# Identity products in TensorE's waits, and one full-array product for the sample rows of a window

## The reference

```
x = x + gt1 * mix
h = rms_norm(x, norm_ffn_w) * (1 + sc2) + sh2
group  = argmax(h @ w_group_router)              # 1 of 4 groups
top-2  = 2 best of the group's 8 experts         # 32 experts in all
y      = sum over the 2 experts of  weight * (silu(h @ gate) * (h @ up)) @ down     # FF = 256
x = x + gt2 * y
out = rms_norm(x, final_norm_w) * (1 + scale) + shift
```

## Time and profile before

| | us |
|---|---|
| median of 3 runs (range) | 838.47 (837.27 to 840.47) |
| profiled execution, its own time | 839.85 |
| span of its trace | 838.1 |
| TensorE busy, share of the span | 728.8, 87% |
| VectorE, ScalarE, GpSimd busy | 264.0, 195.1, 97.5 |
| mean granted TensorE clock | 0.942 |

### The profile page before, as it was taken

The page is one execution under the profiler, slowest core; times in us unless marked ns, Lnnn a source line. Parts: engine busy times, 40 slices in busy tenths (PEclk is TensorE's granted clock), DMA queues, the critical chain, the costliest instruction groups (busy, mean ns, idle before and its releaser), DMA issues.

```text
span 838.1 us, 19950 instructions
## 1 busy us (share of the span) xinstructions
PE 728.8 (87%) x8393; PEld 529.4 (63%) x8394; DVE 264.0 (32%) x737; ACT 195.1 (23%) x500; POOL 97.5 (12%) x229
## 2 busy tenths in 40 slices
PE   2779999999988975998988999973998989999985
PEld 1567777787766654776766777733655656656554
DVE  0145412430134350666683112144111111111122
ACT  1221113112731322122223200051111112121225
POOL 7000000001011222100000000001212221222200
PEclk9869999999999996999998999985899999999996
DMA  7835579999444954651002706875899999999901
GB/s 264 228 103 201 201 245 327 327 327 334 121 112 122 260 148 103 200 179 26 1 2 74 266 0 268 334 300 204 313 413 411 414 413 411 415 412 414 385 15 56
DMA packets 108728, 195.88 MB, mean 234 GB/s; under 512 B 9964, under 2 KB 71097, under 8 KB 100488
## 3 DMA queue, kind: packets, MB, share of 16 engines
q1 hardware_dynamic: 106760, 189.94, 63.1%
q0 software_dynamic: 1920, 5.25, 1.7%
HBM read 185.40 MB, written 9.77 MB: 233 GB/s over the span
## 4 chain that ended last, share of the span: by engine, by line
PE 81%; DVE 6%; DMA 4%; issue 4%; ACT 3%; SPq 1%; POOL 0%; ACTq 0%; DVEq 0%; POOLq 0%
PE ps L1142 17%; PE ps L533 10%; PE ps L1212 7%; PE ps L506 5%; PE ps L546 5%; PE ps L430 4%; PE ps L451 4%; PE ps L1084 4%; PE ps L509 3%; PE ps L434 2%; PE ps L496 2%; DMA arena<-in_w_ada 1%; SPq L811 1%; PE ps L540 1%; DVE arena L1894 1%
## 5 line engine op out<-in xcount | busy, mean ns | idle before, releaser
L1142 PE MATMUL ps<-arena 128*128 128x288 f32 x576 | 144.8, 411 | 0.0
L1142 PEld LDWEIGHTS ps<-arena 128*128 128x128 f32 x576 | 109.3, 192 | 31.2 <-issue 1.0
L533 PE MATMUL ps<-arena 128*32 128x128 f32 x2432 | 86.7, 278 | 15.3 <-issue 12.8
L533 PEld LDWEIGHTS ps<-arena 128*32 128x32 f32 x2432 | 69.3, 111 | 39.4 <-issue 38.2
L1212 PE MATMUL ps<-arena 128*128 128x288 f32 x256 | 76.2, 427 | 14.2 <-DMA arena<-in_w_in 10.3
L1212 PEld LDWEIGHTS ps<-arena 128*128 128x128 f32 x256 | 45.3, 194 | 30.1 <-DMA arena<-in_w_in 10.6
L506 PE MATMUL ps<-level,arena 32*128 32x256 f32 x624 | 44.8, 401 | 0.5 <-DVE arena L775 0.5
L546 PE MATMUL ps<-arena,hact 128*32 128x256 f32 x608 | 40.7, 385 | 0.0
L770 DVE TENSOR_TENSOR h_row<-h_row,ps 128x64 f32<-128x64 f32 x38 | 8.4, 221 | 96.6 <-ACT h_row L628 96.6
L404 POOL DMA_INDIRECT arena<-h_rows,idx_now x38 | 37.6, 988 | 9.5 <-issue 9.5
L1084 PE MATMUL ps<-arena,cT 128*32 128x128 f32 x1024 | 33.8, 292 | 4.6 <-DMA arena<-in_w_ada 4.6
(11 more groups left out here) (432 smaller groups left out, 983.0 us busy)
## 6 DMA issues: line engine op xcount, KB each, us to landing
arena<-in_w_exp_gate SPq DMA_DIRECT2D x32, 1024.0 KB
arena<-in_w_exp_up SPq DMA_DIRECT2D x32, 1024.0 KB
arena<-in_w_exp_down SPq DMA_DIRECT2D x32, 1024.0 KB
arena<-in_w_ada SPq DMA_DIRECT2D x12, 2048.0 KB, 10.2
arena<-in_w_in SPq DMA_DIRECT2D x18, 1024.0 KB, 5.9
arena<-in_w_ada_final SPq DMA_DIRECT2D x4, 2048.0 KB, 14.9
arena<-in_w_in SPq DMA_DIRECT2D x16, 512.0 KB, 4.7
arena<-in_state_ssm_rec SPq DMA_DIRECT2D x8, 512.0 KB, 6.0
```

The source lines that it names most:

```text
L533: l = mm(ps[CW * q:CW * (q + 1), 5, 0:P].rearrange("p (g f) -> p g f", g=2), xwin[:, at:at + CW], gate_up[:, :, k, f:f + HF], start=(k == ...
L1142: l = mm(ps[:, 2 + 2 * sl + m, 0:TOK], w_ring[sl][:, k, m * P:(m + 1) * P], HN[:, k, :], start=(k == 0), stop=(k == KT - 1))
```

## The change

Three edits. A helper busy(n, bank) does n products of the identity with itself taken twice (128 x 128 by 256 columns, fp32) into a bank that nobody reads. It is called before the pair counts (4, after the wait for the last h2_tok, which moves here from below), after the counts (13), after the lists (7), after the last two transposes of y_row (4), and after the final sums of squares (10).

In combined() the four 32 x 32 products of L509 become one product of 128 contraction rows by 128 columns. For that the sample part of PT becomes four times 32 columns, block-diagonal, so PT has 384 columns in place of 288. The table iota has the prompt's numbers, then four blocks of the sample tokens' numbers, in which GpSimd sets to -1 all that is not in a partition of the block's own quarter (two affine_select). The small tables behind them move, and slot_tab takes the place of LG.

```diff
--- before.py
+++ after.py
@@ -267,11 +267,12 @@
         h_row = sb("h_row", [P, HF])
         hact = sb("hact", [P, HF])
         late = level[:].rearrange("p l n -> p (l n)")
-        PT, iota = late[:, 0:TOK], late[:, TOK:2 * TOK]
-        LG = late[:, 2 * TOK:2 * TOK + 108].rearrange("p (t x) -> p t x", t=3)
-        slot_tab = late[:, 2 * TOK + 108:2 * TOK + 108 + 2 * NWIN].rearrange("p (a w) -> p a w", a=2)
-        tid = late[:, 800:806].rearrange("p (c t) -> p c t", c=2)
-        quarter = late[:, 806:807]
+        PTW = SEQ + 4 * SMP
+        PT, iota = late[:, 0:PTW], late[:, PTW:2 * PTW]
+        LG = late[:, 2 * PTW:2 * PTW + 108].rearrange("p (t x) -> p t x", t=3)
+        slot_tab = late[:, 2 * PTW:2 * PTW + 2 * NWIN].rearrange("p (a w) -> p a w", a=2)
+        tid = late[:, 2 * PTW + 108:2 * PTW + 114].rearrange("p (c t) -> p c t", c=2)
+        quarter = late[:, 2 * PTW + 114:2 * PTW + 115]
         idx = sb("idx", [P, NWIN], I32)
         idx_now = sb("idx_now", [P, 2], I32)
         idx_seen = sb("idx_seen", [1, 1], I32)
@@ -389,7 +390,12 @@
             e.wait_ge(S("y_out"), 6)
             e.wait_ge(S("o_out"), 3)
             e.wait_ge(S("x2"), KT)
-            link(g.iota(iota, pattern=[[1, TOK]], base=0, channel_multiplier=0, allow_small_or_imprecise_dtypes=True))
+            link(g.iota(iota[:, 0:SEQ], pattern=[[1, SEQ]], base=0, channel_multiplier=0, allow_small_or_imprecise_dtypes=True))
+            own = iota[:, SEQ:PTW].rearrange("p (m t) -> p m t", t=SMP)
+            link(g.iota(own, pattern=[[0, 4], [1, SMP]], base=SEQ, channel_multiplier=0, allow_small_or_imprecise_dtypes=True))
+            for step, base in ((-SMP, 0), (SMP, SMP - 1)):
+                link(g.affine_select(out=own, in_=own, pattern=[[step, 4], [0, SMP]], base=base,
+                                     channel_multiplier=1 if step < 0 else -1, compare_op=ALU.is_ge, fill=-1.0))
             link(g.iota(tid, pattern=[[0, 2], [P, 3]], base=0, channel_multiplier=1, allow_small_or_imprecise_dtypes=True))
             link(g.memset(LG, 0.0))
             for q in range(4):
@@ -480,6 +486,14 @@
                         l = tr(ps[0:p_, 5, u * 36:(u + 1) * 36], lg_row[:, o_:o_ + p_], ident[0:EG + E, 0:EG + E])
                     l.then_inc(S("rt_mm"), 1)
 
+            def busy(n, bank):
+
+                for _ in range(n):
+                    mm(ps[:, bank, 0:2 * P].rearrange("p (a c) -> p a c", a=2), ident[:, :],
+                       ident[:, :].unsqueeze(1).broadcast_to([P, 2, P]), start=True, stop=True)
+
+            e.wait_ge(S("h2_tok"), 6)
+            busy(4, 7)
             e.wait_ge(S("routed"), 2)
             for t in range(3):
                 for u in range(t):
@@ -488,6 +502,7 @@
             for t in range(3):
                 l = mm(ps[:, 5, 3 * E:4 * E], ones[:, :], r_eq[:, t, :], start=(t == 0), stop=(t == 2))
             l.then_inc(S("count_mm"), 1)
+            busy(13, 7)
 
             def picked_transposed(n):
 
@@ -504,12 +519,9 @@
                     for m in range(4):
                         r = slice(CW * m, CW * (m + 1))
                         mm(ps[:, m, j * SEQ:(j + 1) * SEQ], y_row[r, j * P:(j + 1) * P], PT[r, 0:SEQ], start=False, stop=last and j == 1)
-                for m in range(4):
-                    r = slice(CW * m, CW * (m + 1))
-                    l = mm(ps[r, 4, 0:2 * P], PT[r, SEQ:TOK], y_row[r, :], start=False, stop=last)
+                l = mm(ps[:, 4, 0:2 * P], PT[:, SEQ:PTW], y_row[:, :], start=False, stop=last)
                 l.then_inc(S("comb_mm"), 1)
 
-            e.wait_ge(S("h2_tok"), 6)
             for a in range(2):
                 e.wait_ge(S("placed"), a + 1)
                 for i in range(6):
@@ -517,6 +529,7 @@
                     for q in range(4):
                         l = mm(ps[CW * q:CW * (q + 1), 6 + a, 0:NWIN], B6[0:p, i, :], AV[0:p, a, i, :], start=(i == 0), stop=(i == 5))
                 l.then_inc(S("count_mm"), 1)
+            busy(7, 5)
             picked_transposed(0)
             e.wait_ge(S("comb_mm"), 1)
 
@@ -569,9 +582,11 @@
             for j in range(2):
                 l = tr(ps[:, 5, j * P:(j + 1) * P], y_row[:, j * P:(j + 1) * P], ident[:, :])
             l.then_inc(S("xt_mm"), 1)
+            busy(4, 7)
             for k in range(KT):
                 e.wait_ge(S("x3"), k + 1)
                 mean_square(3, k, 6)
+            busy(10, 7)
             e.wait_ge(S("y_fin"), 1)
             e.wait_ge(S("x_mod"), 3 * KT)
             for t, (o, p) in enumerate(TILES):
@@ -769,7 +784,7 @@
                 e.wait_ge(S("h_silu"), c + 1)
                 tt(h_row[:], h_row[:], ps[:, 5, HF:P], ALU.mult).then_inc(S("h_row"), 1)
                 e.wait_ge(S("comb_mm"), c + 2)
-                ts(PT, iota[:, 0:TOK], slot_tab[:, 0, bass.ds(c, 1)], slot_tab[:, 1, bass.ds(c, 1)], ALU.is_equal,
+                ts(PT, iota, slot_tab[:, 0, bass.ds(c, 1)], slot_tab[:, 1, bass.ds(c, 1)], ALU.is_equal,
                    ALU.mult).then_inc(S("pt"), 1)
                 e.wait_ge(S("down_mm"), c + 1)
                 v.tensor_copy(y_row, ps[:, 7, 0:2 * P]).then_inc(S("y_row"), 1)
```

## The result

The changed kernel takes 841.0 us in the median of 20 runs, the kernel before 838.25 in 20: ratio 1.0031, 95% interval 1.0019 to 1.0043. I forecast 831.0, a gain of 7.5 us, with a range of 826 to 838. It is slower by 2.6 us (1.6 to 3.6). That is less than the 4.2 us that I had set as the least clear difference, so by my own classes it is "within", to which I gave 20%; but the time lies outside my range, and the sign is wrong. They are taken from fast executions alone, which all are but one of full_rows_only's seven, at 1767.13 us.

A forecast was written before the change was run, and what follows sets the result against it. TensorE's chain was taken as the bound, slowed by half-rate clock stretches in the tail. Tables +1.0, held clock -7.25 and sample product -1.2 gave -7.45 us, from 838.47 to 831.0 us; range 826 to 838.

The forecast's parts named there:

- the price of the sample product: L509's replacement in each window: 0.60 us in place of 0.63, a gain of 0.03 in each of 39, 1.2 us.
- the first window: First expert window at full clock: L533 falls from 3.64 to 2.43, gain 1.2 us, and 0.1 from L506.
- L518: no gain: Lists: 35 ns an instruction at half rate against 38 ns for L533 at full rate, so a held clock gains nothing.
- The tables: GpSimd's chain ahead of the router: an iota and two affine_select add 1.0 us, and all the routing moves by that.
- Counts: Pair counts, 18 instructions: 4.05 us at half rate, 1.9 at full rate, a gain of 2.1 us.
- Final norm: Tail end: final squares 6.94 against 4.1, gain 2.8 us; final transposes and copies, gain 0.8 us.
- my first rival: Level falls in the counts all the same: 2.1 us lost, lists 1.8 late, 834.9 us; chance 20%.
- my own upper bound: Sample product in each window: if its weight load doesn't hide, 0.70 us, a loss of 0.07, 2.7 in all.
- the "no gain" that I worked out by it: Sample product by the skill's tiling rule: the drains are as many, the gain is nothing, 832.2 in place of 831.0 us.
- My other bound: Sample product: if the weight load hides entirely, it costs only 0.46 us, up to 0.13 gained, 5.1 in all.
- the cover is ... the gather: Identity products cost nothing at full rate, covered by VectorE's routing work, the gather, the root and the modulation.
- my second rival: Ahead of the router: the level's rise of 557.0 comes later, L468 ends 3.9 us late, 833.9 us; chance 10%.

The follow-up runs named there:

- full_rows_only: Kernel before with one edit: L462 takes all 128 contraction rows of y_row and xT in place of 32; 837.14 us, ratio 0.9952.
- load_and_tables: Changed kernel with expert 6's down weights loaded after the gathered rows are copied and the new tables made behind the clearing of y_row; 834.75 us, ratio 0.9962.
- fills_loop: Kernel before with all 38 identity products as counted loops, old sample product, tables and load order; 837.37 us, ratio 0.9977.
- load_after_gather: Changed kernel in which SP asks for expert 6's down weights only when ScalarE has copied the first gathered rows; 838.55 us, ratio 0.9989.
- tables_late: Changed kernel with GpSimd's three new table instructions moved behind the clearing of y_row; 839.01 us, ratio 1.0016.
- fills_only: Kernel before with all 38 identity products written out, old sample product and tables; 870.65 us, ratio 1.0377.
- product_only: Changed kernel without its five busy() calls: full-array sample product, wider PT and tables only; 842.66 us, ratio 1.0057.
- fills_loop_load: Kernel before with all 38 identity products as counted loops, expert 6's down weights asked for after the first gathered rows are copied; 832.92 us, ratio 0.9933.

## Why the prediction was wrong

Three steps failed: the price of the sample product; the first window, whose gather I took as fixed cover; and, behind that, "L518: no gain". The tables were a little too cheap as well.

**Right.** In the changed kernel's trace the identity products hold the level and fit (0.45 each where I had 0.46). Counts: forecast -2.1, measured -1.9 up to the lists. Final norm: forecast -3.6, measured -3.9 in the pair of traces, but 3.1 on average over all traces. That the level held through the routing is in part luck. Of the eight traces with all 38 products it did so in three (after, load_and_tables, fills_loop). In three it fell for 3.4 us some 2.3 to 2.9 us after the counts began (load_after_gather, tables_late, fills_only), as my first rival had it (20%); it cost 0.44 us and not 3.9, because the counts were over and only some of the 13 products were slow. In two it fell later, once in the lists and once ahead of the first window.

**The sample product** was the step that failed in every window. I took 0.60 us against 0.63 from a pair of full-array instructions that stand between full-array ones. Between tiled ones it took 0.70, my own upper bound: 39 x 0.07 = +2.7 (2.5 with the unrounded 0.065) where I had -1.2, an error of 3.9 us. product_only shows it without the rest. The weights of that pair began to load at 522.25, 0.24 us ahead of it, while the product before still ran; here the weight load starts with the product, both at 809.09:

```profile
522.25 0.43 PEld L442 LDWEIGHTS ps<-arena,ones 128*128 128x128 f32 x2
```
```profile
809.09 0.30 PEld L522 LDWEIGHTS ps<-arena,level 128*128 128x128 f32 x2 [0.33 <-issue]
```

The Trainium skill ("TensorEngine Tiling (Array Packing)", Key Properties) says that changing the tiling mode drains TensorE; the "no gain" that I worked out by it was nearer than my row. No run shows a drain apart from the weight load. My other bound was a slip: 0.63 - 0.46 is 0.17 a window, not 0.13.

**The first window** was to gain 1.6 (first window 1.3, transposes 0.25); it lost 2.6. The failed step is "the cover is ... the gather": I had costed the gather as fixed. A faster TensorE signals the lists' end sooner, SP's wait for it ends sooner, and 1 MB goes ahead of the gather. That SP waits for count_mm was in the code and I named only TensorE's and VectorE's queues. load_after_gather took it back: 3.5 us. A second pair, fills_loop and fills_loop_load, gives 3.7.

**The lists** were to gain nothing from the level. I compared L518 at half rate (35 ns an instruction, 52 columns) with L533 at full rate (38 ns, but 128 columns). At full rate L530 takes 24 ns an instruction (2.26 / 96). That brought the gather 0.5 us forward, and it is also what set the load free 1.9 us sooner and so ahead of the gather.

**The tables.** Forecast +1.0 for the longer chain; L468 starts 1.2 later (the two affine_select take 0.76 where I had 0.58), and product_only and load_after_gather have the counts 1.2 to 1.3 late. The traced execution of the changed kernel had 4.1, near the 3.9 of my second rival (10%). But there the level had fallen before L468 began, which that rival did not have, so the match of the size is luck. How late the router starts changes from one execution to the next. In the eight traces with 32 rows in L462 and no new tables ahead of it, it starts 6.9 to 7.5 us after the first table in six and at 9.8 and 9.9 in two (tables_late, fills_loop_load); in the three with the tables at 9.1, 9.2 and 11.2.

In sum, from the forecast of -7.5: product +3.9, gather and first window +4.2, tables +0.3, final norm and lists -0.6 make +0.3, and with the late level of that execution +2.8 the trace's 3.0. The timing says +2.6 (1.6 to 3.6). The late level is not the changed kernel's own (3 of the 11 traces have it, with the tables and without), so it can't be counted on to fill the 2.3 us between that and +0.3. The final norm on average (3.1 in place of 3.9) fills 0.8; the other 1.5 stay open.

**Not foreseen at all** is what decided whether the change could be made: code. Written out, the identity products alone cost 31 us. So the sample product, a loss of 2.5 to 2.7 us in the windows and of 4.8 (2.9 to 6.7) with its tables, is in this change also what keeps the loop's code loaded.

**Open.** The identity products by themselves (fills_loop) bring 1.9 us (0.8 to 3.1). The account of its trace against that of the kernel before is -3.9 (final norm) - 2.4 (up to the gather) + 2.3 (gather to first window) = -4.0, and with the final norm's average gain of 3.1 it is -3.2, still a little beyond the interval. The loop also varies: from the first window to the last copy it takes 224.9 us in the trace of the kernel before, and 225.8 to 226.8 in the four others with the old product, none of fills_only's pauses and the first window at 3.64. The kernel before's trace is the shortest there and the longest in the final norm; why executions differ in the loop I don't know.

## What to carry to other kernels

Before you make one engine faster ahead of a small urgent DMA, look for every queue that waits on the same semaphore: a large transfer that it releases may now go first. Count the code that you add ahead of a loop of many copies, look at the page's row of instruction loads, and use a counted loop for fillers. Price an instruction from a row that has the same shape and the same neighbours. And before you explain a single trace, read the same stretch in every trace that has the same code there: here the final norm alone differs by 2.2 us between executions.

## What the runs showed of the hardware

- With ten fp32 instructions on 32 of 128 contraction rows the granted clock fell although TensorE was busy; with the same ten on 128 rows it held (L462: 5.36 against 4.13 us, and L468 behind it 6.18 against 4.04). It fell in or just before L462 in eleven traces of eleven with 32 rows, and in none of three with 128.
- Identity products in the waits held the level through the final norm in nine traces of nine (22.0 us), and through routing and lists only in some; where it fell, 13 products took 7.54 us in place of 5.86.
- Without them the final norm took 23.7 to 25.9 us with the same code.
- A full-array fp32 product of 256 columns between tiled groups took 0.70 us, four diagonal 32 x 32 ones side by side 0.63, all 39 of them in the trace of either kernel.
- 96 instructions more in TensorE's program, executed long before the loop, made each jump back of a loop of 7 window copies some 10.5 us longer (17.3 against 6.8), of which 8.3 are pauses and 2.3 the clock that fell in them.
- A gather issued 0.1 us behind 1 MB of weights was copied 5.3 to 5.5 us after its issue, 2.3 to 2.5 later than one issued ahead of them.
- VectorE's write of PT went from 0.43 to 0.48 us for 384 columns in place of 288, where I had expected 0.57.
